# Forming a latent unit's weights ahead of the next unit's first dot, in a kernel whose engines follow a written order

## The reference

```
ue = jnp.take(u_tab, it, axis=0)          # one 4 KB row for each token and expert
ve = jnp.take(v_tab, it, axis=0)
a = jax.nn.gelu(jnp.einsum('td,ted->te', xt, ue))
return jnp.einsum('te,ted->td', gt * a, ve)
```

## Time and profile before

| | |
|---|---|
| median of 3 runs | 4175.05 us (4171.27 to 4175.13) |
| the profiled execution | 4185.1 us, its span 4183.0 us |
| busy share of the span | PE 76%, DVE 69%, POOL 61%, PEld 36%, ACT 25% |
| moved by DMA | 1485.65 MB, 355 GB/s over the span; 1342.34 MB of it are expert rows |

### The profile page before, as it was taken

One profiled execution on the slowest core, in us unless ns is written; L12 is line 12 of the kernel. 1 busy time (PEld: TensorE's weight loads), 2 busy tenths in 40 slices (PEclk: granted clock), 3 DMA queues, 4 the chain that ended last, 5 costly groups with the idle time before them and its releaser, 6 DMA issues.

```text
span 4183.0 us, 34218 instructions
## 1 busy us (share of the span) xinstructions
PE 3164.1 (76%) x9936; PEld 1485.0 (36%) x9936; DVE 2897.0 (69%) x6522; ACT 1061.0 (25%) x2249; POOL 2558.9 (61%) x2564
## 2 busy tenths in 40 slices
PE   6898883289877777787777887867777777777777
PEld 4655551145422222232222446432222222222223
DVE  2378896846666667888765988876666666666662
ACT  4333421133221222222221325112122222222222
POOL 0054565635667677666777756666666666766674
PEclk8899995689999999999999999989999999999999
DMA  7586789899999999989999987899999999999998
GB/s 283 213 309 244 247 322 397 306 388 364 411 368 386 399 382 388 382 331 381 391 395 403 370 323 262 317 336 378 384 384 372 387 383 381 396 385 382 384 382 310
DMA packets 394007, 1485.65 MB, mean 355 GB/s; under 512 B 44124, under 2 KB 46878, under 8 KB 377952
## 3 DMA queue, kind: packets, MB, share of 16 engines
q0 software_dynamic: 368640, 1342.34, 83.9%
q1 hardware_dynamic: 25184, 141.13, 8.7%
HBM read 1480.42 MB, written 2.88 MB: 355 GB/s over the span
## 4 chain that ended last, share of the span: by engine, by line
PE 26%; DMA 26%; POOL 19%; issue 13%; DVE 12%; ACT 4%; SPq 0%; ACTq 0%; DVEq 0%; POOLq 0%
POOL rows_ring L681 19%; DMA rows_ring<-in_peer_u,idx 15%; PE psum L999 11%; DMA rows_ring<-in_peer_v,idx 7%; PE psum L770 6%; DVE rows_ring L1585 5%; DVE mix L1600 2%; PE psum L900 2%; DMA rows_ring<-in_peer_v,idx_c 1%; DMA rows_ring<-in_peer_u,idx_c 1%; PE psum L757 1%; PE psum L891 1%; PE psum L913 1%; ACT area L1221 1%; DMA ring<-in_ada 1%
## 5 line engine op out<-in xcount | busy, mean ns | idle before, releaser
L999 PE MATMUL psum<-rows_ring,diag 128*128 128x512 f32 x4096 | 2081.2, 644 | 797.3 <-DMA rows_ring<-in_peer_v,idx 475.1
L1585 DVE SCALAR_TENSOR_TENSOR rows_ring<-rows_ring,psum 128x1024 f32<-128x1024 f32 x1024 | 1247.8, 1219 | 783.0 <-DMA rows_ring<-in_peer_u,idx 757.8
L999 PEld LDWEIGHTS psum<-rows_ring,diag 128*128 128x128 f32 x4096 | 756.6, 200 | 2077.7 <-DMA rows_ring<-in_peer_v,idx 1057.7
L681 POOL DMA_INDIRECT rows_ring<-in_peer_v,idx x1024 | 976.8, 954 | 608.1 <-PE psum L999 357.6
L681 POOL DMA_INDIRECT rows_ring<-in_peer_u,idx x1024 | 979.0, 956 | 389.5 <-issue 266.9
L1249 ACT ACTIVATE diag<-ident,wts 128x128 f32<-128x128 f32 x1024 | 389.0, 398 | 1570.6 <-PE psum L999 1567.4
L681 POOL DMA_INDIRECT rows_ring<-in_peer_u,idx_c x256 | 316.1, 1235 | 444.7 <-DVE idx_c L1572 210.9
L770 PE MATMUL psum<-area,ring 128*128 128x128 f32 (+2 forms) x1600 | 388.4, 404 | 5.4 <-ACT area L1095 4.8
L681 POOL DMA_INDIRECT rows_ring<-in_peer_v,idx_c x256 | 286.8, 1120 | 158.2 <-DVE mix L1600 83.3
L1585 DVE SCALAR_TENSOR_TENSOR rows_ring<-rows_ring,area 128x1024 f32<-128x1024 f32 x256 | 312.4, 1221 | 53.0 <-DMA rows_ring<-in_peer_u,idx_c 51.8
L1600 DVE SCALAR_TENSOR_TENSOR mix<-rows_ring,wts,mix 128x1024 f32<-128x1024 f32 x254 | 326.1, 1284 | 16.6 <-DMA rows_ring<-in_peer_v,idx_c 15.1
(11 more groups left out here) (205 smaller groups left out, 2393.3 us busy)
## 6 DMA issues: line engine op xcount, KB each, us to landing
ring<-in_ada SPq DMA_DIRECT2D x48, 1024.0 KB, 8.5
ring<-in_win SPq DMA_DIRECT2D x32, 1024.0 KB, 8.0
ring<-in_wout SPq DMA_DIRECT2D x16, 1024.0 KB, 8.2
ring<-in_wq SPq DMA_DIRECT2D x16, 1024.0 KB, 8.0
rows_ring<-in_peer_u,idx POOLq DMA_INDIRECT x1024, 6.6
rows_ring<-in_peer_v,idx POOLq DMA_INDIRECT x1024, 6.6
ring<-in_dft SPq DMA_DIRECT2D x12, 1024.0 KB, 8.0
rows_ring<-in_peer_u,idx_c POOLq DMA_INDIRECT x256, 6.5
```

The source lines that it names most:

```text
L681: pool.indirect_dma_start(row(table, k), None, (peer_u, peer_v)[table], bass.IndirectOffsetOnAxis(ap=idx_of(grp, u)[:, k:k + 1], axis=0)). ...
L999: m = pe.matmul(acc[:, b, :], diag[:, k % 4, :], row(1, k)[:, b * 512:(b + 1) * 512], start=(u % PEER_HEADS == 0 and k == 0), stop=last)
L1585: dve.scalar_tensor_tensor(out=row(0, k), in0=row(0, k), scalar=1.0, in1=h, op0=ALU.mult, op1=ALU.mult, accum_out=dots[(u + UNIT0[grp]) % ...
```

## The change

In a step whose previous unit is a latent one, `weigh` of that unit is put ahead of dot 0 of the new unit, where it stood behind it. Context units keep the old order. The turns of PE, ACT and DVE and two of the banks are written anew. POOL's loop is written with one counter, which runs v rows `UP_BEHIND` (16) fetches of u behind u rows.

```diff
+UP_BEHIND = TOPK
+WEIGH_EARLY = (L_,)
...
+    early = prev and GROUPS[prev[0]][1] in WEIGH_EARLY
+    jobs += [("weigh", *prev, 0)] if early else []
     for p in range(PIECES):
         jobs += [("dot", *cur, p)] if cur else []
         if p == 0:
-            jobs += [("weigh", *prev, 0)] if prev else []
+            jobs += [("weigh", *prev, 0)] if prev and not early else []
             jobs += [("gexp", *cur, 0)] if cur and cur[0] not in PICKED_AHEAD else []
         jobs += [("add", *prev, p)] if prev else []
...
-            for i in range(len(ALL_UNITS) + 1):
-                if i < len(ALL_UNITS):
-                    pool.wait_ge(s["idx_ready"], PICK[ALL_UNITS[i]] + 1)
-                for k in range(TOPK):
-                    if i < len(ALL_UNITS):
-                        fetch(0, *ALL_UNITS[i], k)
-                    if i > 0:
-                        fetch(1, *ALL_UNITS[i - 1], k)
+            for j in range(len(ALL_UNITS) * TOPK + UP_BEHIND):
+                if j < len(ALL_UNITS) * TOPK:
+                    if j % TOPK == 0:
+                        pool.wait_ge(s["idx_ready"], PICK[ALL_UNITS[j // TOPK]] + 1)
+                    fetch(0, *ALL_UNITS[j // TOPK], j % TOPK)
+                if j >= UP_BEHIND:
+                    i = j - UP_BEHIND
+                    fetch(1, *ALL_UNITS[i // TOPK], i % TOPK)
```

More of the change, by code:

```diff
@@ L346 @@
     "75647564756475647564756475647523642375647564756423756423756423756423756423756423756423756423756423756423756475"
-    "647564756475647564756746574623572346235746")
+    "647564756475647564756476574623572346235746")
 def in_turns(turns):
```

## The result

The changed kernel takes 4076.32 us in the median of 4 runs (4074.74 to 4079.51), the kernel before on the same chip 4173.16 us (4163.46 to 4175.13). The ratio is 0.9773, with a 95% interval of 0.9757 to 0.9790: 97 us or 2.3% faster. The forecast was 4042 us, 34 us too low, in a range of 4000 to 4115 that holds the time.

A forecast was written before the change was run, and what follows sets the result against it. It took the wait for PE's late, cold first add at each step boundary, which runs the DMA engines dry, as the bound. 127 us from steps plus 6 from mixer stretches made 133: 4042 us against the median, range 4000 to 4115.

The forecast's parts named there:

- The chain at the boundary: After a unit's last dot (end L), `weigh` ends 2.30 us earlier, PE's first add starts at L+2.83, POOL's 3.26 us wait goes.
- What a step costs without the wait: Steps of expert work alone fall from 43.66 to 41.3 us; 54 x 2.36 = 127 us saved.
- The base of 41.0: Step cost without the wait, from step 40's 40.95 us at 409 GB/s, taken as held throughout.
- The tiles' ends: Two steps after each tile's end, DVE's wait for PE's transposes stays: 1.5 us in 6 steps, 0.17 us a step.
- POOL's own pace: POOL needs 1.21 us a fetch with its issue, 38.8 us for a step's 32, so it isn't the bound.
- The reference point: The 133 us gain was taken off the 4175 us median, giving 4042; the profiled execution took 4185.1 us.
- Mixer stretches: In steps 8 to 14, four boundaries gain 2.3 us and two late ones lose about 3: 6 us, between -6 and 27.
- turns: Rewritten order of PE, ACT and DVE jobs: mixer jobs move by one or two adds or dots, a chain shifting once.
- POOL's loop: With 16 fetches behind, the one-counter loop issues the same list as before: zero.
- B: Rival: the u ring becomes the wait and steps stay at 42.7 us; 58 us saved, 4117 us; 14 in 100.
- A: Rival: transfers are hidden anyway or at their ceiling; steps keep 43.66 us, 4175 us; 7 in 100.
- C: Rival: `weigh` blocks DVE until a late gelu, delaying dot 0 by 2.4 us; up to 130 us lost, 4305 us; 4 in 100.

The follow-up runs named there:

- e1: The kernel before with only `weigh` of latent units moved ahead of dot 0, old turns, banks and POOL loop kept: 4079.42 us, ratio 0.9771.
- e2: The changed kernel with `weigh` ahead of dot 0 only up to step 15 and in steps 30 to 32: 4157.3 us, ratio 0.9979.
- e3: The kernel before with `gexp` behind the fourth expert's diags in the last group's units from the third on: 4122.77 us, ratio 0.9869.
- e8: The kernel before with three extra matmuls ahead of a unit's first add, in the last group except tiles' first units: 4139.36 us, ratio 0.9910.
- e4: The changed kernel with `gexp` behind the fourth expert's diags in all latent units: 4060.25 us, ratio 0.9734.
- e9: The kernel of e4 with u rows fetched at half length and dots over 512 elements in units 48 to 79: 4013.14 us, ratio 0.9625.
- run 97: Not a run's label: the 97 us gain of the changed kernel's median, 4076.32 us, against the kernel before, 4173.16 us.
- e6: The changed kernel with two extra VectorE multiplications between `weigh` and dot 0 in steps 49 to 78: 4070.49 us, ratio 0.9763.
- e7: The changed kernel with six extra VectorE multiplications between `weigh` and dot 0 in steps 49 to 78: 4095.04 us, ratio 0.9826.

## Why the prediction was right, and what it mis-sized

**The chain at the boundary: right.** `weigh` at L+0.60 (L+0.61 said), the add at L+2.82 (L+2.83), 0.73 us of idleness (under 1 us), a warm add (1.96 us for 1.98), dot 0 still when its row lands. e1 and e2 show that the moved job is the cause; e3 and e8 show which part of the chain pays: the start of the first add, and for half of it or more its clock.

**What a step costs without the wait: the term that was mis-sized.** The text said 41.3 us, measured were 41.75, which over 53 steps is the 24 us by which 101.4 fall short of 53 x 2.36 = 125. Two parts make it up. *The base of 41.0* came from the one step 40. The 46 ordinary steps have 41.42 us in the mean, 0.3 above the 41.13 said for them; most of them come at 40.8 to 41.0 or at 41.5 to 42, and step 40 was of the shorter kind. Its 409 GB/s isn't held: 403 to 405 is the most that any run showed over 30 steps. *The tiles' ends* were put at 0.17 us a step, and the seven steps there are 2.4 us longer than the others, 7 x 2.4/53 = 0.32. Here the place was right and the reason wrong: the text blamed DVE's wait for the transposes, which hardly changes (28.7 us over the seven tile ends from step 17 to 73, 33.3 before). The larger loss is `close` and `gexp` ahead of the first diag on ACT, and e4 takes 1.6 of the 2.4 us away. The earlier trace rows could have told: its dry window 3138 to 3146 lies behind just such a boundary, 56/57. It was read as the loss at every boundary, which by luck is nearly right: behind the ordinary boundary 57/58 the windows of the kernel before are

```profile
3180.00:3184.00 4.00, 4.00 (x9) 1.73 (x8) 2.67 (x5) 0.79 (x2) 1.71 (x2) 0.77 0.96 367
3184.00:3188.00 4.00, 4.00 (x11) 1.66 (x10) 2.51 (x9) 0.82 (x3) 2.98 (x4) 1.00 0.91 295
3188.00:3192.00 4.00, 1.99 (x5) 0.68 (x4) 1.23 (x2) 0.40 (x1) 2.89 (x4) 1.00 0.93 322
```

which are 4 x (42 + 114 + 87)/409 = 2.4 us of lost transfer. What was saved is 2.1 us at the ordinary steps (43.5 to 41.42) and 0.7 at the seven (44.5 to 43.8).

**POOL's own pace: put too low.** The prediction's 38.8 us a step counts POOL's gap ahead of a fetch only where the row says issue, but every fetch has one. With 0.947 us for the fetch and 0.303 for the gap it is 40.0 us for 32, and e9 shows 40.1. POOL still wasn't the bound at 43.7, but the 41.0 taken as the base lies only 1 us above its pace, so that there was less room under the forecast's 41.0 to 42.2 than the text thought.

**The reference point: 10 us of the miss.** The 133 us were worked out from steps of an execution that itself took 10 us more than the median of 4175, and then taken off that median: 4175 - 133 = 4042. The changed kernel's profiled execution shows no such 10 us (4076.75 us, median 4076.32), so profile against profile the gain is 108 us and run against run 97. Of the 34 us by which the forecast was too low, 25 are the sum's (133 said, 108 measured), nearly all of them the steps', and the rest is this.

**Mixer stretches, turns, POOL's loop.** 8 us saved in steps 8 to 14 for 6 said, but by another cause: e1 has the early `weigh` there and no gain, so the new turns are needed, which had been put at zero. The text rightly saw gelu late there but not that the turns bring it forward; that the number fits is luck. The other stretches sum to -3.4 us for the zero said (3.0 - 2.3 - 0.5 - 3.6), inside the 10.

**The rivals.** *B*, the u ring: POOL's wait for dots didn't grow (21.2 to 20.5 us), and in e6 and e7 a slack near the 2.15 taken fits the growth of that wait. *A*, transfers at their ceiling: 403 GB/s at a DMA share hardly changed. The 358 GB/s for a core that the prediction cites from the Trainium skill ("DMA: Bandwidth & Descriptors", section "Where 436 GB/s comes from") doesn't bind in this case. The Trainium skill's page "HBM Reference" (section "Specifications (TRN2)") says that a core that streams alone measures about 425 GB/s; the 403 to 410 seen here stand nearer to that. *C*, gelu late: it wasn't in steps of expert work, and e7 shows that even a dot 0 that is 3.6 us late costs only 0.6 to 0.8 us a step.

**Not settled:** why most ordinary steps fall into two kinds some 0.8 us apart, and why the turns' part in steps 8 to 14 shows in e2's median (6.7 us below before) but not in e1's against the changed kernel. It is no larger than what the kernels' starts differ by: the first dot of the context comes at 212.4 to 221.7 us in the twelve profiles, with old turns and new.

## What to carry to other kernels

Where an engine's share says "full", look at the rate beside it at the boundary of a loop, and follow the instruction that restarts there: here it was late by 2.3 us and started cold, and being cold was worth at least as much as being late. When a row says that an engine waited, take off the pause that it makes ahead of every instruction of that kind. Take the new base of a loop from a stretch of many steps, never from the single step that happens to lack the wait, and look at boundaries of each kind (here a tile's end) before one of them is taken for all. When a job is moved out of the way of a critical one, read what else stands ahead of it on that engine's list: the COPY and the table load left at the tiles' ends were worth another 11 to 18 us.

## What the runs showed of the hardware

The lower of TensorE's two clock levels at a loop's restart cost 1.0 to 1.5 us in each of 30 steps of a kernel in which TensorE isn't the bound, and three extra matmuls got that back (e8). With a ring of four places a consumer's start could slip by 0.65 us at no cost (e6) and by 3.6 us for 0.6 to 0.8 (e7). And 32 gathers of 128 rows took 40.1 us even with a quarter of the bytes left out (e9), so the bytes, with half of each dot, were worth only 1.4 us of a step of 41.5. POOL also pauses for 1.4 to 2 us with nothing that the profile shows to wait for (2.01 us ahead of a v row at 3615.20 us in the changed kernel): six times in the 30 steps of the changed kernel, about 138 us or twice that apart, and never in those of before, of e7 and of e9. No run tells the cause.
